# TensorE makes eight of the sixteen opening modulation tiles; the opening's steps on VectorE and ScalarE are reordered

## The reference

```python
ada_lat = silu(c) @ w_ada[l] + b_ada[l]        # and the same for c_ctx: 9 * 1024 numbers each
n = rmsnorm(h, norm_g) * (1 + sc) + s          # s, sc, g: ninths of ada
h = h + 0.5 * g * swiglu(n, w_up, w_down)      # first and third sub-step
...
h = fftconv: rfft(filter), filter = mlp(features) * decay / l1 norm   # a part of the second sub-step
```

## Time and profile before

| | us |
|---|---|
| median of three runs | 3253.15 (3249.09 to 3253.91) |
| the profiled execution's own time | 3254.8 |
| its span, first to last instruction | 3252.9 |
| TensorE busy | 3127.1 (96%) |
| VectorE busy | 1755.3 (54%) |
| ScalarE busy | 973.6 (30%) |
| first feed-forward matmul starts | 103.12 |

### The profile page before, as it was taken

The page is one execution under the profiler, slowest core; times in us unless marked ns, Lnnn a source line. Parts: engine busy times, 40 slices in busy tenths (PEclk is TensorE's granted clock), DMA queues, the critical chain, the costliest instruction groups (busy, mean ns, idle before and its releaser), DMA issues.

```text
span 3252.9 us, 48065 instructions
## 1 busy us (share of the span) xinstructions
PE 3127.1 (96%) x20628; PEld 3040.0 (93%) x20628; DVE 1755.3 (54%) x2911; ACT 973.6 (30%) x1472; POOL 46.1 (1%) x89
## 2 busy tenths in 40 slices
PE   6799999998999999999999999998999999999998
PEld 3799999987999999999999999997789989999998
DVE  5655756646555655343465565665555545642334
ACT  2322222314444432121242121233244433322222
POOL 0000000000000000000000000000000000000000
PEclk8899999999999999999999999998899999999999
DMA  7255533464222523232223343251712252322221
GB/s 275 78 195 209 217 144 117 188 231 179 79 77 96 216 78 131 90 117 91 104 91 124 123 155 143 104 218 69 278 70 82 73 194 103 112 96 78 78 74 64
DMA packets 76278, 426.30 MB, mean 131 GB/s; under 512 B 8657, under 2 KB 12177, under 8 KB 44066
## 3 DMA queue, kind: packets, MB, share of 16 engines
q1 hardware_dynamic: 58656, 325.08, 27.0%
q0 software_dynamic: 9168, 53.61, 4.3%
q10 hardware_dynamic: 8242, 44.53, 3.4%
HBM read 369.03 MB, written 54.17 MB: 130 GB/s over the span
## 4 chain that ended last, share of the span: by engine, by line
PE 80%; DVE 10%; ACT 4%; issue 3%; DMA 3%; DVEq 0%; ACTq 0%; SPq 0%
PE tile_psum L544 37%; PE tile_psum L551 19%; PE tile_psum L929 5%; PE tile_psum L505 3%; PE tile_psum L470 3%; PE tile_psum L933 3%; PE misc_psum L470 2%; PE tile_psum L510 2%; PE tile_psum L758 1%; ACT whi L1162 1%; DVE wlo L1659 1%; DMA raw<-in_w_mix 1%; PE tile_psum L980 1%; DVE n_lo L1737 1%; DVE h L1815 1%
## 5 line engine op out<-in xcount | busy, mean ns | idle before, releaser
L544 PE MATMUL tile_psum<-n_hi,whi 128*128 128x320 f32 x3264 | 745.0, 309 | 3.6 <-DVE n_lo L1737 3.0
L544 PE MATMUL tile_psum<-n_lo,whi 128*128 128x320 f32 x3264 | 742.2, 308 | 0.0
L1659 DVE TENSOR_TENSOR wlo<-raw,whi 128x2048 fp32r<-128x2048 f32 (+2 forms) x202 | 444.6, 2201 | 204.2 <-ACT whi L1162 201.2
L544 PEld LDWEIGHTS tile_psum<-n_hi,whi 128*128 128x128 f32 x3264 | 544.4, 188 | 8.1 <-DVE n_lo L1737 6.1
L544 PEld LDWEIGHTS tile_psum<-n_lo,whi 128*128 128x128 f32 x3264 | 545.4, 188 | 0.0
L551 PE MATMUL tile_psum<-n_hi,wlo 128*128 128x320 f32 x3264 | 512.3, 308 | 0.0
L551 PEld LDWEIGHTS tile_psum<-n_hi,wlo 128*128 128x128 f32 x3264 | 486.8, 188 | 0.0
L1162 ACT ACTIVATE whi<-raw 128x2048 fp32r<-128x2048 f32 (+2 forms) x202 | 370.4, 1834 | 370.7 <-DMA raw<-in_w_up 178.7
L544 PE MATMUL tile_psum<-x_hi,whi 128*128 128x320 f32 x1408 | 320.6, 308 | 0.0
L544 PE MATMUL tile_psum<-x_lo,whi 128*128 128x320 f32 x1408 | 320.3, 308 | 0.0
L1261 ACT ACTIVATE gate_act<-tile_psum 128x320 f32<-128x320 f32 x176 | 76.8, 437 | 702.4 <-PE tile_psum L551 702.3
(11 more groups left out here) (313 smaller groups left out, 3790.5 us busy)
## 6 DMA issues: line engine op xcount, KB each, us to landing
raw<-in_w_up SPq DMA_DIRECT2D x88, 1024.0 KB, 4.8
w_ada<-in_w_ada SPq DMA_DIRECT2D x128, 512.0 KB, 5.7
raw<-in_w_down SPq DMA_DIRECT2D x32, 1024.0 KB, 4.8
raw<-in_w_gate SPq DMA_DIRECT2D x24, 1024.0 KB, 4.8
whi<-table_keep SPq DMA_DIRECT2D x20, 1024.0 KB, 4.8
wlo<-table_keep SPq DMA_DIRECT2D x20, 1024.0 KB, 7.0
g_keep<-gate_out POOLq DMA_DIRECT2D x48, 320.0 KB, 2.5
gates<-g_keep POOLq DMA_DIRECT2D x16, 960.0 KB, 6.1
```

The source lines that it names most:

```text
L544: pe.matmul(tps[:, t.s, m, 0:TH], blk(p, m * n + k)[0], (hi, lo)[b][:, k, tok], start=k == 0 and b == 0, stop=False)
L1659: dve.tensor_tensor(wlo[:, r, 0:cols], raw[:, r, 0:cols], whi[:, r, 0:cols].bitcast(F32), ALU.subtract)\
```

## The change

`ADA_DOTS` goes from 12 to 8. VectorE makes tiles 0 to 7, TensorE tiles 8 to 15: the row products are 16 matmuls in place of 8, in four pieces of weights (two of the eight row blocks, 1024 wide, 1 MB each) in place of two (four row blocks, 512 wide, 1 MB each). `w_ada_rows` keeps its size, so that pieces 2 and 3 take the places of 0 and 1, and SyncE waits on the new semaphore `rows_used` before it loads them; what stands behind on its queue waits too. The first piece's matmuls stand behind `mlp(1)`, the other three between taps. Eight small turns take the place of four. VectorE's tiles are steps of the list alone (before, some were inside `first_taps`). The squares go one by one, the stores of frequencies (`kept`) and the rounding of the first two panels (`panel`) become steps of their own, later or earlier than before.

```diff
-ADA_DOTS = 12
+ADA_DOTS = 8
...
-FIRST_ORDER = [("taps", 0, t) for t in range(5)] + [("taps", 1, 0), ("turned",), ("taps", 1, 1)]
+FIRST_ORDER = [("taps", 0, 0), ("rows", 1), ("taps", 0, 1), ("ada",), ("taps", 0, 2), ("rows", 2), ("taps", 0, 3), ("ada",), ("taps", 0, 4)]
+FIRST_ORDER += [("rows", 3), ("taps", 1, 0), ("rows_out",), ("taps", 1, 1), ("filter", 0, 0), ("turned",), ("taps", 1, 2), ("ada",)]
...
             mlp(0, ft0, mz0)
+            mlp(1, ft0, mz0)
             rows = taken(slots.tile())
             pe.wait_ge(cols_on, 1)
...
+            def row_products(i):
+
+                pe.wait_ge(piece_in[i], 16)
+                for k in (2 * i, 2 * i + 1):
+                    for bank in range(2):
+                        ins = pe.matmul(tps[0:2, rows.s, bank, :], ccs[:, 2 * k:2 * k + 2], pieces[:, k % 4, bank * 512:(bank + 1) * 512],
+                                        start=k == 0, stop=k == KT - 1)
+                if i == 3:
+                    ins.then_inc(rows.done, 1)
+                else:
+                    ins.then_inc(rows_used, 1)
...
             row_products(0)
-            mlp(1, ft0, mz0)
-            row_products(1).then_inc(rows.done, 1)
...
-            for half in range(2):
-                sp.dma_start(pieces[:, 4 * half:4 * half + 4, :], w_first[4 * half:4 * half + 4].rearrange("k p c -> p k c"))\
-                    .then_inc(piece_in[half], 16)
-                ada_load(1)
-            ada_load(2)
+            for i in range(4):
+                if i > 1:
+                    sp.wait_ge(rows_used, i - 1)
+                sp.dma_start(pieces[:, 2 * i % 4:2 * i % 4 + 2, :], w_first[2 * i:2 * i + 2].rearrange("k p c -> p k c"))\
+                    .then_inc(piece_in[i], 16)
+                if i < 2:
+                    ada_load(1 + i)
+            ada_load(1)
...
-                elif (o, t) == (1, 4):
-                    round_panel()
-                    round_panel()
...
-                elif o or t % 2:
-                    ada_step(1)
```

More of the change, by code:

```diff
@@ L349, in program @@
         hi_ready, lo_ready = sem("panel_hi_ready"), sem("panel_lo_ready")
-        early_in, piece_in = [sem(f"ada_early_in{k}") for k in range(4)], [sem(f"ada_rows_in{k}") for k in range(2)]
+        early_in, piece_in = [sem(f"ada_early_in{k}") for k in range(4)], [sem(f"ada_rows_in{k}") for k in range(4)]
+        rows_used = sem("ada_rows_used")
         cols_in, cols_on, turned_out, w3_in = sem("c_cols_in"), sem("c_cols_silu"), sem("ada_turned"), sem("w3_in")
@@ L698, in turn_rows @@
                 m = misc()
-                for i in range(4):
+                for i in range(8):
                     ins = pe.matmul(mps[:, m, 0, 2 * i:2 * i + 2], ada_rows[:, i * P:(i + 1) * P], ident[0:2, 0:2], start=True, stop=True)
@@ L709, in nothing @@
                 pass
-            first = {"combine": nothing, "add_squares": nothing, "ada": nothing, "taps": lambda o, t: raw_taps(o, t, hid20), "norms": lambda o: l1_norms((ab0, ab1)[o]),
+            first = {"combine": nothing, "add_square": nothing, "ada": nothing, "kept": nothing, "rows_out": nothing, "panel": nothing,
+                     "rows": row_products, "taps": lambda o, t: raw_taps(o, t, hid20), "norms": lambda o: l1_norms((ab0, ab1)[o]),
                      "filter": first_filter, "sums": first_sums, "turned": turn_rows}
@@ L1317, in first_combine, with one_square, first_panel @@
                     act.dma_start(fq_keep[o, f + 2 * half], fqp[:, f, half, :]).then_inc(fq_kept[f], 16)
-            def add_squares(m0, m1):
-                for m in range(m0, m1):
-                    next_square(m)
-                if m1 == KT:
+            def one_square(m):
+                next_square(m)
+                if m == KT - 1:
                     due(sq_used)
+            def first_panel():
+                round_panel()
+                round_panel()
             def next_square(m):
@@ L1789, in ada_step @@
                         tiles_done[0] = ADA_EARLY
+                        dve.wait_ge(ada_used, ADA_DOTS)
                         dve.sem_inc(ada_used, ADA_EARLY - ADA_DOTS)
-                    if tiles_done[0] % 8 == 0 and tiles_done[0] > made[0]:
-                        made[0] = tiles_done[0]
+                    while made[0] + 8 <= tiles_done[0]:
+                        made[0] += 8
                         section((made[0] - 1) // ADA_TILES, (made[0] - 1) % ADA_TILES // 8)
@@ L1989, in first_combine, with one_square @@
                 both_halves(first_slots[o, f], fqp[:, f, 0, :], fqp[:, f, 1, :])
-            def add_squares(m0, m1):
-                for m in range(m0, m1):
-                    add_square()
-                if m1 == KT:
+            def one_square(m):
+                add_square()
+                if m == KT - 1:
                     dve.sem_inc(sum_ready, 1)
```

33 lines of the change are left out of this document (15 added, 18 removed).

## The result

The changed kernel takes 3257.55 us (median of 17 runs, 3253.22 to 3263.37) against 3250.58 us before (17 runs beside it, 3246.65 to 3256.23): a ratio of 1.0023, interval 1.0015 to 1.0030. It is about 7 us slower where 3 us less were predicted. Its profiled execution took 3257.23 us, with a span of 3255.4.

What follows compares the result with a forecast made beforehand. Bound by TensorE after 103 us, so only the opening counts: `filter(1, 0)` starting 0.35 earlier and 3.1 shorter, less 0.2 behind, puts the first normalised row 3.1 earlier; 3253.15 - 3.1 = 3250.0 us, range 3245.5 to 3254.5.

Steps and rivals of the forecast that it cites:

- the first paragraph: Whole kernel: TensorE is busy 3068.8 of 3149 us from 103 us on, so what moves in the opening reaches the end one for one.
- The one that was slower: Opening: piece 2 lands as late as piece 1 did, 17.4 us, costing 7.3 us: 3260.4 us; chance 0.05.
- the sign that would refute the paragraph: Behind the opening: a difference in the stretch from the first normalised row to the end; no size given.
- First tap at 28.5: Opening: VectorE's first tap comes at 28.5 us instead of 31.98, 3.5 us earlier.
- Idle 3.5 us before the second tap: Opening: VectorE idles some 3.5 us before `taps(0, 1)` at 32.9, since rows 1 stand ahead of it on TensorE.
- Piece 2 lands 7 us after its request: Opening: piece 2, requested at 27.5, takes 7 us to land, so rows 2 can start at 34.5.
- filter(1, 0) at full clock, 3.65: Opening's tail, TensorE: this filter takes 3.65 us instead of 6.75, from 60.3 to 64.0.
- Norms 5.6, filter(1, 1) 5.75, ending at 75.3: Opening's tail, TensorE: norms take 2.4 and 3.2 us, then the filter 5.75, ending at 75.3 instead of 78.65.
- The rival with a clock that stays up: Opening's tail: full clock through norms and `filter(1, 1)`, a gain of 6.2 us, or 6.8: 3246.3 to 3247; chance 0.18.
- Waits of 5.7, 3.8 and 3.1 before the first, the third sum and behind the panels: Opening's tail: VectorE idles some 5.7 us before the first sum, 3.8 before the third, 3.1 behind the panels.
- First normalised row 3.1 us earlier: End of the opening: VectorE's first normalised row comes at 98.1 us instead of 101.17.
- What stands behind is as before: Behind the opening: the rest keeps its length, so the opening's gain of 3.1 us reaches the end whole.

Runs made afterwards that it cites:

- before_pe48: The kernel before with 48 semaphore increments that nobody reads on TensorE ahead of its first matmul: 3258.88 us, ratio 1.0023 to the kernel before.
- after_pe208: The changed kernel with 208 semaphore increments on TensorE in the opening, 128 of them ahead of its first matmul: 3259.49 us, ratio 1.0024 to the kernel before.
- after_fit208: The changed kernel with 208 semaphore increments on TensorE where it waits anyway (36, 72 and 100): 3250.05 us, ratio 0.9999 to the kernel before.
- after_2k: The changed kernel with the pieces laid out in DRAM in 2 KB rows instead of 4 KB: 3258.85 us, ratio 1.0020 to the kernel before.
- before_both: The kernel before with 48 semaphore increments on TensorE and 107 on VectorE ahead of its first wait: 3259.80 us, ratio 1.0028 to the kernel before.
- before_pe128: The kernel before with 128 semaphore increments on TensorE, 28 ahead of its first matmul and 100 ahead of the token sums: 3250.53 us, ratio 0.9997.
- the last two fillings: The changed kernel with 208 or 80 semaphore increments on TensorE where it waits anyway: 3250.05 and 3248.53 us.
- after_fit80: The changed kernel with 80 semaphore increments on TensorE ahead of the token sums, where it waits: 3248.53 us, ratio 0.9993 to the kernel before.
- again_before: The kernel before, unchanged, run and profiled again beside itself: 3250.27 us, ratio 1.0002.

## Why the prediction was wrong

The step that failed is in the first paragraph: "whatever the change does, it does before, in the opening, and what it moves there reaches the end one for one". The opening did come out earlier, and the rest did not stay as long as it was: 12 matmuls more in the opening moved TensorE's later fetches, two of them into loads of layer 0's mixing that are waited for, and the mixing grew by 5.6 us between the first two pairs of profiles, by 6.4 between the middle ones of five with before's count (682.5) and of five of the changed kernel (688.9). None of the rivals had it. The one that was slower (3260.4, a chance of 0.05) is near the measured 3257.55 by luck: it has TensorE idle before L692 for a late piece, and in the changed kernel TensorE is not. The last part of the prediction did name the sign that would refute the paragraph, and that sign came. Shown: that the loss comes of TensorE's instruction count, and so of where its later fetches fall, and that it goes with it (before_pe48, after_pe208, after_fit208). Read from two loads, and only argued for the rest: that each part of it is a fetch in a load's way. That the clock falls because TensorE then waits is not shown.

By its own steps:

- *First tap at 28.5*: 31.43. The sine came at 21.71, not 19.06, since the pieces' longer rows slow ScalarE's queue (the prediction took the start as unchanged); with 2 KB rows the tap was at 28.71 and the next at 33.22 (foreseen: 28.5 and 32.9). The order was right, and a transfer's price in its neighbours was left out.
- *Idle 3.5 us before the second tap*: 3.82.
- *Piece 2 lands 7 us after its request*: 5.9 in the changed kernel, where it was asked for 2.8 us later than foreseen; in after_2k, asked for at 27.04 (foreseen: 27.5), rows 2 came 9.6 us behind the request. They started at 36.7 either way, not at 34.5, which is about what the opening's gain lacks.
- *filter(1, 0) at full clock, 3.65*: 3.72. *Norms 5.6, filter(1, 1) 5.75, ending at 75.3*: 5.21, 6.36, 77.16. The rival with a clock that stays up did not come: the granted clock was full to 69.4 and then at its lower level. (The working calls its 2.4 and 3.2 us of the norms "the same"; by rows 6 and 7 it is some 3.0 at the full clock and 2.8 at the lower one, 5.80 in all.)
- *Waits of 5.7, 3.8 and 3.1 before the first, the third sum and behind the panels*: 4.34, 4.63, 2.91.
- *First normalised row 3.1 us earlier*: in six profiles with before's opening (before_pe48, before_both and before_pe128 among them) it came at 98.95 to 102.01, middle 101.2; in six of the changed kernel's with 4 KB rows (the last two fillings included) at 98.34 to 100.02, middle 99.6. A gain of about 1.6, from ranges that overlap.
- *What stands behind is as before*: wrong; the whole loss of 7 us lies there, and the opening's gain with it. With this undone, after_fit208 takes 3250.05 and after_fit80 3248.53 against 3250.72: 0.7 and 2.2 us less, which is the 1.6 of the opening as far as medians tell, and within 0.2% of no change.

**Still open.** Behind the two loads VectorE waits 3.3 us longer in before_pe48 than in again_before (6.36 for 4.02 and 6.38 for 5.44); what makes up the rest of the loss, other fetches or the clock, was not traced one by one. Why layer 1's mixing, whose fetches move by as many instructions, keeps its length is not known. after_fit80 had also the shortest of these, 694.5 us against 698 to 702, in one profile, which may be its fetches or chance.

## What to carry to other kernels

A change in instruction count on an engine with a long unrolled program moves every later fetch of that program; where loads are waited for just in time, that alone was worth some 0.2% here, over twice what the change was forecast to bring. Before a small gain or loss is put down to the work, compare the stretches behind the change, and repeat the old kernel with the new one's instruction count: 48 idle instructions in a wait did it. And price a transfer's shape by what it takes from the other queues: 4 KB rows on one queue held an issue on the other up for 2 to 3 us.

## What the hardware showed unexpectedly

- TensorE's program came in 163 packets of 16 KB during the run. Where one started 5.0 to 5.5 us into a certain 1 MB load, the load landed after 5.7 to 7.5 us instead of 4.9 to 5.5: in six of eight profiles the last of its 16 packets of 4 bytes stood behind the fetch, when all its data packets had started.
- A semaphore increment on TensorE took 127 ns (80 in 10.13 us).
- A queue whose rows are 4 KB instead of 2 KB takes a larger share: ScalarE's issue beside it took 11.17 to 11.85 us (ten profiles) against 8.57 to 9.32 (eight).
- Profiles of the same opening ended 3 us apart (98.95 to 102.01), more than the effect that was looked for there.
